# A two-layer mixer kernel on one core: the first layer's modulation in two groups of four channel blocks

## What is computed

```python
shift, scale, gate = jnp.split(silu(c) @ w_mod[l] + b_mod[l], 3, axis=-1)  # once for latent, once for context
h = x * (1 + scale) + shift
proj = h @ w_in[l]                       # the first 1,536 columns are hy_in
hid = sin(sf[0] * (feats @ w1 + b1)); hid = sin(sf[1] * (hid @ w2 + b2))
filt = (hid @ w3) * exp(-t * exp(log_decay))          # long filters, 2 orders, 2 directions
u = short_conv(hy_in)                    # three taps along the tokens
z = gate * irfft(rfft(z) * rfft(filt))   # twice, and so on
```

## Time and profile before

| | |
|---|---|
| median of 3 runs | 1951.15 us (1946.24 to 1952.62) |
| profiled execution | 1950.17 us |
| its span, first to last instruction | 1948.4 us |
| TensorE matmul busy | 1817.4 us (93%) |
| VectorE busy | 1133.0 us (58%) |
| ScalarE busy | 664.3 us (34%) |
| GpSimd busy | 456.7 us (23%) |
| granted TensorE clock, mean | 0.979 of full |
| moved by DMA | 150.00 MB, 77 GB/s mean |

### The profile page before, as it was taken

One profiled execution on the slowest core, in us unless ns is written; L12 is line 12 of the kernel. 1 busy time (PEld: TensorE's weight loads), 2 busy tenths in 40 slices (PEclk: granted clock), 3 DMA queues, 4 the chain that ended last, 5 costly groups with the idle time before them and its releaser, 6 DMA issues.

```text
span 1948.4 us, 27784 instructions
## 1 busy us (share of the span) xinstructions
PE 1817.4 (93%) x11336; PEld 1580.1 (81%) x11336; DVE 1133.0 (58%) x1582; ACT 664.3 (34%) x1148; POOL 456.7 (23%) x210
## 2 busy tenths in 40 slices
PE   5999999999999999999969999999999999999995
PEld 3787899886877777999856969997878677789995
DVE  5599893545243444486877989825434444435834
ACT  3424312444224444212243342234433344442121
POOL 0100032212230111467211001322223211115650
PEclk8999999999999999999979999999999999999998
DMA  8110021211310111354520102211122011115331
GB/s 342 44 54 33 33 98 60 65 38 45 114 44 20 33 33 39 123 191 142 208 87 33 55 33 76 77 60 50 44 79 79 22 36 33 34 44 187 128 109 54
DMA packets 48493, 150.00 MB, mean 77 GB/s; under 512 B 9386, under 2 KB 10922, under 8 KB 47600
## 3 DMA queue, kind: packets, MB, share of 16 engines
q1 hardware_dynamic: 44768, 134.09, 19.7%
q10 hardware_dynamic: 3600, 14.16, 2.1%
HBM read 141.63 MB, written 6.59 MB: 76 GB/s over the span
## 4 chain that ended last, share of the span: by engine, by line
PE 69%; DVE 22%; ACT 4%; issue 4%; DMA 1%; POOL 1%; SPq 0%; ACTq 0%; DVEq 0%; POOLq 0%
PE PS L798 16%; PE PS L803 15%; PE PS L799 15%; PE PS L852 4%; PE PS L841 3%; PE PS L1101 2%; PE PS L886 2%; PE PS L883 2%; PE PS L1034 2%; PE PS L865 2%; DVE Wl L1467 1%; DVE st L1446 1%; DVE MG L1697 1%; DMA pmod_w<-in_w_mod 1%; PE PS L1090 1%
## 5 line engine op out<-in xcount | busy, mean ns | idle before, releaser
L1857 POOL TENSOR_TENSOR Wl<-W,Wh 128x1024 fp32r<-128x1024 f32 (+1 forms) x166 | 375.1, 2261 | 1343.3 <-ACT Wh L1152 1263.0
L798 PE MATMUL PS<-Hh,Wh 128*128 128x320 f32 x2048 | 612.7, 314 | 16.8 <-ACT Wh L1152 8.9
L799 PE MATMUL PS<-Hl,Wh 128*128 128x320 f32 x2048 | 604.4, 310 | 0.0
L798 PEld LDWEIGHTS PS<-Hh,Wh 128*128 128x128 f32 x2048 | 386.2, 189 | 41.1 <-issue 26.4
L799 PEld LDWEIGHTS PS<-Hl,Wh 128*128 128x128 f32 x2048 | 386.6, 189 | 0.6 <-issue 0.5
L803 PE MATMUL PS<-Hh,Wl 128*128 128x320 f32 x2048 | 321.4, 310 | 0.9 <-POOL Wl L1857 0.9
L803 PEld LDWEIGHTS PS<-Hh,Wl 128*128 128x128 f32 x2048 | 305.5, 188 | 1.4 <-POOL Wl L1857 1.4
L1446 DVE TENSOR_REDUCE st<-PS 128x1 f32<-128x640 f32 (+1 forms) x160 | 114.9, 718 | 318.6 <-PE PS L865 176.0
L1152 ACT ACTIVATE work<-PS 128x640 f32<-128x640 f32 (+9 forms) x298 | 172.5, 592 | 257.7 <-PE PS L803 68.3
L1152 ACT ACTIVATE Wh<-W 128x1024 fp32r<-128x1024 f32 x196 | 184.9, 948 | 60.1 <-PE PS L803 26.8
L1289 ACT ACTIVATE th<-PS 128x640 f32<-128x640 f32 x64 | 45.1, 705 | 367.3 <-PE PS L803 367.3
(11 more groups left out here) (211 smaller groups left out, 2487.4 us busy)
## 6 DMA issues: line engine op xcount, KB each, us to landing
W<-in_w_in SPq DMA_DIRECT2D x132, 512.0 KB, 3.5
W<-in_w_branch SPq DMA_DIRECT2D x48, 256.0 KB, 2.6
work<-in_w_mod_rows ACTq DMA_DIRECT2D x23, 512.0 KB, 3.7
pmod_w<-in_w_mod SPq DMA_DIRECT2D x8, 1024.0 KB, 12.9
W<-in_w_out SPq DMA_DIRECT2D x16, 512.0 KB, 4.1
late_modulation_w<-in_w_mod_rows SPq DMA_DIRECT2D x9, 512.0 KB, 5.7
work<-in_x_sample SPq DMA_DIRECT2D x2, 2048.0 KB
x_mid<-work SPq DMA_DIRECT2D x1, 2560.0 KB, 8.5
```

What stands on the lines that cost most here:

```text
L798: pe.matmul(out, Wh[:, b, kk, :], xh[:, kk, t], start=kk == 0, stop=False)
L799: pe.matmul(out, Wh[:, b, kk, :], xl[:, kk, t], start=False, stop=False)
L1857: return pool.tensor_tensor(out, in_, high.bitcast(f32), ALU.subtract)
```

## The change

The columns of the first modulation are laid out anew, so that one transfer brings shift and scale of one channel block, and one `pmrow` serves two blocks. Two `pmrow`/`pmod` pairs come first; blocks 0 to 3 then need only these. The second two pairs lie among the chunks, as do `ffn` 1 and filters 0 and 1; filters 2 to 4 go among `conv` 0 to 3, and the five `fdft` behind them. The exponentials of the log decays (`first_decay`) move from the step `lam` to filter 0, in layer 0 only. The buffers of the modulation weights are four instead of five, and lie in other areas. SP's order of transfers becomes: four modulation transfers, tokens, first two weight tiles, the other four, filter weights and decays; then a wait for `pmrow` 2, and the forward tables. VectorE makes the low parts of weights 0 and 1 at block 2, and the low parts `Hl` of layer 0 in pairs, at the odd blocks.

```diff
@@ def layer_steps(l):
     if l == 0:
-        p = [("pmod", g) for g in range(4)]
-        f = [("ffn", 0), ("ffn", 1)] + [("filt", t) for t in range(NT)] + [("fdft", i) for i in range(5)]
-        rows = [("pmrow", g) for g in range(4)]
-        s = [("lam", 0)] + f[:1] + rows[:1] + f[1:2] + rows[1:2] + p[:1] + rows[2:3] + p[1:2] + f[2:4] + rows[3:] + p[2:3]
-        s += f[4:5] + p[3:] + start_steps([], {2: f[5:6], 4: f[6:7]})
-        s += [("conv", 0), ("conv", 1), ("fdft", 0), ("fdft", 1), ("conv", 2), ("fdft", 2), ("conv", 3), ("fdft", 3), ("fdft", 4)]
+        f = [("filt", t) for t in range(NT)]
+        s = [("lam", 0), ("ffn", 0)]
+        s += [("pmrow", 0), ("pmod", 0), ("pmrow", 1), ("pmod", 1)] + [("ht", c) for c in range(4)]
+        s += [("two", 0), ("ffn", 1), ("two", 1), ("two", 2), ("pmrow", 2), ("pmod", 2), ("pmrow", 3), ("pmod", 3)]
+        s += [("ht", 4), ("two", 3), ("ht", 5), ("two", 4), ("ht", 6), ("two", 5)] + f[:1] + [("ht", 7), ("two", 6)] + f[1:2] + [("two", 7)]
+        s += f[2:3] + [("conv", 0), ("conv", 1)] + f[3:4] + [("conv", 2)] + f[4:] + [("conv", 3)]
+        s += [("fdft", i) for i in range(5)]
...
-NP = 5
+NP = 4
...
-        table[l, STEPS[l].index(("ht" if l == 0 else "lam", 0))] = 2
+        table[l, STEPS[l].index(("lam", 0) if l else ("ht", 2))] = 2
...
-        pmod_w = sb("pmod_w", [128, NP, 2, KD, 128], over=Hh_at)
-        cpad = sb("cpad", [128, KD, 32], over=Wl_at)
...
+        cpad = area(work, 20000, KD, 32)
+        pmod_w = [area(MG, 2048 * n, 2, KD, 128) for n in range(2)] + [area(work, 13328 + 2048 * n, 2, KD, 128) for n in range(2)]
...
             layer_tables(0, 0)
             for g in range(2):
                 first_modulation(g)
-            layer_tables(0, 1)
-            for g in range(2, NP):
+            for g in range(2, 4):
                 first_modulation(g)
             load_x(0)
-            for g in range(NP, KD):
-                first_modulation(g)
             weight(0)
             weight(1)
+            for g in range(4, KD):
+                first_modulation(g)
+            layer_tables(0, 1)
+            sp.wait_ge(*filled(0, "pmrow", 2))
             layer_tables(0, 2)
...
+            def first_decay(l):
+
+                act.wait_ge(filter_here, 16 * N_FILTER * (l + 1))
+                link(act.activation(expld, expld, ACT.Exp))
+                act.activation(decay, expld[:, :, 0, :], ACT.Exp, scale=negt[:, 0:1]).then_inc(sems["decay_ready"], 1)
...
-                        act.wait_ge(filter_here, 16 * N_FILTER * (l + 1))
-                        link(act.activation(expld, expld, ACT.Exp))
-                        act.activation(decay, expld[:, :, 0, :], ACT.Exp, scale=negt[:, 0:1]).then_inc(sems["decay_ready"], 1)
+                        if l:
+                            first_decay(l)
...
+                        if i == 0 and l == 0:
+                            first_decay(l)
...
-                            m = 4 * i + j
+                            m = 2 * i + j // 2 + KD * (j % 2)
...
-                        if i == 0:
+                        if l == 0 and i == 2:
+                            low_part(l, 0)
+                            low_part(l, 1)
+                        if l == 0 and i % 2 == 0:
+                            dve.wait_ge(*after("ss_ready", l, 2 * i + 4))
+                        elif i == 0:
                             dve.wait_ge(*after("ss_ready", l, 2 * KD))
...
-                        if l == 0 and i < 2:
-                            low_part(l, i)
-                        for c in [i - 1] * (i > 0) + [i] * (i == KD - 1):
+                        for c in [i - 1] * (i > 0) + [i] * (i == KD - 1) if l else (i - 1, i) if i % 2 else ():
```

More of the change, by code:

```diff
@@ L661, in first_modulation @@
                     sp.wait_ge(*filled(0, "pmrow", (g - NP) // 2))
-                sp.dma_start(pmod_w[:, g % NP], A["w_mod"][0, 2 * g:2 * g + 2].rearrange("m p k n -> p m k n"))\
+                sp.dma_start(pmod_w[g % NP], A["w_mod"][0, 2 * g:2 * g + 2].rearrange("m p k n -> p m k n"))\
                   .then_inc(pmod_here[g % NP], 16)
@@ L900, in _ @@
                                 last = pe.matmul(ps[32 * j:32 * j + 32, 0:128], cpad[:, k, :],
-                                                 pmod_w[:, (2 * i + j // 2) % NP, j % 2, k, :], start=k == 0, stop=k == KD - 1)
+                                                 pmod_w[(2 * i + j // 2) % NP][:, j % 2, k, :], start=k == 0, stop=k == KD - 1)
                         last.then_inc(full_of(l, kind, i), 1)
@@ L1478, in _ @@
             dve.wait_ge(c_sig, 1)
-            link(dve.memset(cpad[:], 0.0))
+            link(dve.memset(cpad, 0.0))
             TT(cpad[:, :, 0:2], ccol[:], csig, ALU.mult).then_inc(c_silu, 1)
@@ L1949, in laid_out @@
         "w3": x["hy_ffn_w3"].reshape(DEPTH, HY_FFN, 2, 2 * HY).transpose(0, 2, 1, 3).reshape(DEPTH, 128, 2 * HY),
-        "w_mod": tiles(x["w_mod"][0:1, :, 0:2 * D]),
+        "w_mod": tiles(x["w_mod"][0:1, :, 0:2 * D]).reshape(1, 2, KD, 128, KD, 128).transpose(0, 2, 1, 3, 4, 5).reshape(1, 2 * KD, 128, KD, 128),
         "w_mod_rows": np.concatenate([x["w_mod"][0, :, 2 * D:], x["w_mod"][1, :, 0:2 * D], x["w_mod"][1, :, 2 * D:]], -1)
```

## The result

The changed kernel takes 1954.2 us (median of 20 runs, 1950.25 to 1955.97), the kernel before beside it 1947.95 (median of 20, 1946.04 to 1952.95). The ratio is 1.0027 with a 95% interval of 1.0020 to 1.0034: about 5.2 us slower, 3.9 to 6.6. The profiled execution took 1954.14 us with a span of 1952.3, against 1950.17 and 1948.4.

The account below looks back on a forecast made before the run. Transfers were taken to bound the kernel to about 44 us, then a VectorE, ScalarE and TensorE relay up to line 1615. Terms -9.1 + 6.2 + 4.1 = +1.2 us on the 1951.15 median gave 1952.3, range 1945 to 1958.

Parts of the forecast that it names:

- Leg 1: Start to block 4's modulation: fewer weights ahead of the tokens bring it from 55.58 to 46.5 us, gain 9.1.
- Leg 2: Block 4's modulation to the first projection's copy: first_decay and filter 0 now stand in the way, 16.37 to 22.6, loss 6.2.
- The 1.7 us that I took for the clock: From two 6 on: TensorE's clock falls to half after some 6 us idle, costing about one chunk, 1.7 us.
- Leg 3: First projection's copy to VectorE's long spectrum chain (line 1615): 40.31 becomes layer 1's 44.43 us, loss 4.1, bounds 0 to 4.1.
- the lost cover: Between first copy and line 1615: two fdft no longer fill TensorE's wait for ScalarE's copies; part of the 4.1 us.
- the filters' matmuls: Between first copy and line 1615: filters' matmuls, formerly past by then, now fall there; part of the 4.1 us.
- Clock at half from the tokens to two 7: Slower rival: TensorE stays at half clock from the tokens to two 7, +9.7 us, 1961; chance 0.15.
- The cover holds: Faster rival: second group and filters hide wholly, TensorE alone sets the time up to the first copy; -16, 1935; chance 0.12.
- Leg 3 free: Rival: the stretch from first copy to line 1615 loses nothing; -2.9 us, 1948.2, no change; chance 0.06.

Follow-up runs that it names:

- e11: The changed kernel, unchanged, profiled a second time; block 4 modulated at 46.51 us, long spectrum chain starting at 116.55 us.
- e2: The changed kernel with ffn 1 moved into the wait for the tokens; one execution took 1955.18 us.
- e1: The changed kernel with the exponentials of the log decays moved ahead of block 4; 1950.56 us, ratio to the kernel before 1.0006.
- e3: The changed kernel with 42 unread transposes keeping TensorE busy in the gap ahead of two 6; one execution took 1952.83 us.
- e5: The changed kernel with unread transposes ahead of two 6 and ahead of the matmuls of filters 2 and 3; one execution took 1953.08 us.
- e6: The kernel before with only the five fdft moved behind conv 3; one execution took 1953.01 us.
- e7: The changed kernel with ffn 1, late modulations, decays, filters 0 to 2 and table transfers reordered at once; 1943.78 us, ratio to the kernel before 0.9970.
- e9: The kernel before, unchanged, profiled again; 1947.0 us, in the lower group of its times.
- e10: The kernel before, unchanged, profiled again; 1951.49 us, in the upper group of its times.

## Why the prediction was right, and where it was short

**Leg 1: the time right, the path in part.** The tokens landed at 23.3 (forecast 22.3 to 23.2), and block 4 came at 47.06 and 46.51 (46.5). The queue that the prediction named, ffn 1 on VectorE, then ScalarE's sine, copy, pmrow 3, copy, is the last to end in e11. In the first profile it isn't: TensorE, at half until 39, ended `pmrow` 2 about 0.6 us behind the sine, though the prediction said that the chunks and this row cost nothing there. That the two paths came out so near each other wasn't forecast, so the time of the first profile is right by some luck. e2 shows the same from the other side: with the whole step gone block 4 gained 3.6 us, not the 5.8 of the chain and the sine.

**Leg 2: right in size and mostly in cause.** +6.3 against +6.2 (22.9 in both profiles of after, 16.6 the mean of before's five). The gap was 6.53 us (some 6), and two 6 ran at half. The 1.7 us that I took for the clock measured 1.5. e1 shows that first_decay, with its share of the clock, carries 3.8 of it.

**Leg 3: the direction and the comparison with layer 1 were right, the size was not.** The term was mis-sized: 4.1 forecast as the upper bound, 5.5 and 6.9 measured. I took layer 1's stretch as the upper end, with the clock that it has there. In before's layer 1 the clock holds, and TensorE waits ahead of one filter only:

```profile
1025.44 1.25 PE L948 MATMUL PS<-BR 64*128 64x512 f32 x4 [1.36 <-ACT raw L1152]
```

(PEclk is 1.00 over 1021 to 1067.) Here it waits 1.44 and 1.36 us ahead of two filters, and the clock falls, with the 6.5 us ahead of two 6 (after) or without them (e3). What in these waits decides it no run shows. e5 takes the fall away and gets 44.41: the transferred 4.1 is right at full clock. The prediction gave two reasons for it, the lost cover and the filters' matmuls; by e6 the filters are the larger, an estimated 3.3 of the 4.1.

**Sum.** Predicted -9.1 + 6.2 + 4.1 = +1.2. The two profiles of after against the mean of the five of before give -9.5 + 6.3 + 6.2 = +3.0 (long chain at 116.2 and 113.1). That is 0.2 above the upper end of +2.8 that the forecast gave. The other 2 us of the 5.2 must lie behind the long chain, where the prediction said that nothing moves: the work doesn't, its clock does. The profiles show 0.9 of them (a rest of 1835.7 for the two of after, 1834.8 for the five of before); the remainder is inferred from the timed runs. That the total came within 2 us of the forecast's 1952.3 is in part luck: that number was made on a median of three runs of which two were of the upper group; against 1947.95, +1.2 would be 1949.2, and the measured time is 5 above that.

**Rivals.** *Clock at half from the tokens to two 7* didn't come: it was full from 39 to 59. But its mechanism, TensorE at half holding block 4, is what the first profile shows up to 39, and leg 3 paid a little of its price. *The cover holds* failed for the stated reason: first_decay stands in an in-order queue ahead of a needed step (e1), and so does ffn 1's chain, though TensorE's own work was nearly as late (e2). e7, which moves both and more, gets 10.5 of the 16 us that the rival named (long chain at 102.59 against 113.1). *Leg 3 free* didn't come: leg 3 lost 5.5 and 6.9. The decays' table load cost its 1.28 us and the next ACTIVATE started 0.02 us later, so the extra drain that the Trainium skill ("ScalarE: Activation LUTs", What ACT_TABLE_LOAD costs) names doesn't show at this place either.

## What to carry to other kernels

Moving work out of a transfer-bound stretch is a gain only as far as each instruction's in-order queue lets it be: list, for each moved step, what stands behind it on its own engine and who waits for that, and put it where that engine has a wait anyway (ffn 1 under the tokens, the decays ahead of `pmrow` 3's row copy in e7). Price a TensorE gap twice, once for its length and once for the clock behind it. Where totals lie in groups, take several profiles and compare stages; a single total can hide a 4 us difference in work that nobody changed.

## What the runs showed of the hardware

- A gap on TensorE of 6.5 us cost a further 1.5 us in slower matmuls behind it. Two waits of 1.4 us, 1.2 us of work apart, cost 1.4 and 2.8 in the two profiles of after and 2.5 in e3, where the gap ahead of them was filled. Transposes that nobody reads, put into the gaps, held the granted clock at the full level (2.4 GHz) and took that price away (leg 2 22.91 to 21.38, leg 3 46.87 to 44.41).
- The same waits at the same place in the same kernel may or may not be followed by a fall to the half level (1.2 GHz): PEclk 1.00 in e9 and 0.68 in e10 between 480 and 490 us. Over the profiles the untouched part of the run lasted 1832.1 to 1840.8 us, the longest where the clock fell most often (e2); the table of losses above speaks for the clock as the reason, but e5 doesn't fit it and no run tested it.
- Leg 3 of before was 40.30 or 40.31 us in all five profiles, at a granted clock of 1.00 throughout: here, where the clock held, a stage of 40 us repeated to a hundredth.
